# A two-block transformer layer on one Trainium2 core: squares summed on VectorE, narrow weights stationary in four column groups, router products between the last projection's units

## The reference

```
h = rmsnorm(x, norm_mix_g);  z = h @ w_in          # among its columns 8 + 8 narrow ones, a and b
g_log = -exp(a_log) * softplus(a + dt_bias);  beta = sigmoid(b)      # gated delta rule, latent attention
x = x + merged @ w_out
h = rmsnorm(x, norm_ffn_g)                                           # "norm_ffn"
x = x + (silu(conv(gate)) * conv(up)) @ w_down
x = rmsnorm(x, norm_final_g)                                         # "norm_final"
h = rms_norm(x, norm1_g);  proj = h @ w_in_2       # among its columns 32 narrow ones, dt
...                                                                  # state-space branch, windowed attention
x = x + merged @ w_out_2
h2 = rms_norm(x, norm2_g)
logits = h2 @ [w_router_group, w_router_expert]                      # 8 + 64 = 72 columns
...                                                # best group, two of its experts, 64 experts in all
x = x + sum over chosen experts of gate * ((silu(h2 @ w_gate_e) * (h2 @ w_up_e)) @ w_down_e)
```

## Time and profile before

| | |
|---|---|
| time, median of 3 runs | 1587.01 us (1586.24 to 1587.95) |
| the profiled execution's own time | 1585.9 us |
| its span, first to last instruction | 1584.0 us |
| mean granted TensorE clock | 0.98 |
| PE busy | 1487.1 us (94%) |
| DVE busy | 512.3 us (32%) |
| ACT busy | 333.8 us (21%) |
| DMA | 347.31 MB, mean 219 GB/s |

### The profile page before, as it was taken

How to read it: one execution, slowest core, us unless ns; L and a number is a source line. 1 busy time by engine, 2 the same in 40 slices (tenths; PEclk the granted TensorE clock), 3 DMA queues, 4 the chain that set the end, 5 groups by cost and what they waited for, 6 DMA issues and landing times.

```text
span 1584.0 us, 29393 instructions
## 1 busy us (share of the span) xinstructions
PE 1487.1 (94%) x12766; PEld 1257.9 (79%) x12766; DVE 512.3 (32%) x1255; ACT 333.8 (21%) x737; POOL 3.8 (0%) x6
## 2 busy tenths in 40 slices
PE   8999989999999999899999999997999888797988
PEld 7868879978888888787788888887777667576756
DVE  1435064221244420218753551013322222122212
ACT  1152321331100000112435531001111111111111
POOL 0000000000000000000000000000000000000000
PEclk9999999999999999999999999997999999999999
DMA  8333424224344324344334444393999999999992
GB/s 315 127 109 131 159 85 150 81 80 160 133 148 146 132 104 165 155 146 148 107 107 147 146 134 145 120 372 121 418 419 420 419 419 420 420 419 420 419 419 88
DMA packets 58334, 347.31 MB, mean 219 GB/s; under 512 B 12416, under 2 KB 13536, under 8 KB 18656
## 3 DMA queue, kind: packets, MB, share of 16 engines
q1 hardware_dynamic: 55536, 339.11, 55.3%
q10 hardware_dynamic: 2672, 6.33, 1.1%
HBM read 413.13 MB, written 1.49 MB: 262 GB/s over the span
## 4 chain that ended last, share of the span: by engine, by line
PE 84%; DMA 7%; DVE 4%; issue 2%; ACT 1%; SPq 0%; DVEq 0%; ACTq 0%
PE bank L375 34%; PE bank L988 9%; PE bank L419 8%; PE bank L389 6%; PE bank L1008 5%; DMA work<-w_gate_e_dram 5%; PE bank L1019 4%; PE bank L1032 3%; PE bank L435 2%; DVE work L1616 2%; DMA ring<-w_gate_e_dram 2%; PE bank L351 1%; PE bank L522 1%; PE bank L478 1%; PE bank L881 1%
## 5 line engine op out<-in xcount | busy, mean ns | idle before, releaser
L375 PE MATMUL bank<-hT,ring 128*128 128x256 f32 x2080 | 460.6, 382 | 3.4 <-DVE hT L1616 3.4
L375 PEld LDWEIGHTS bank<-hT,ring 128*128 128x128 f32 x2080 | 396.2, 192 | 63.8 <-issue 10.4
L1625 DVE TENSOR_TENSOR xT<-xT,bank 128x512 f32<-128x512 f32 x100 | 68.7, 687 | 349.6 <-PE bank L1008 231.4
L375 PE MATMUL bank<-work,ring 128*128 128x256 f32 x640 | 139.1, 379 | 0.0
L375 PEld LDWEIGHTS bank<-work,ring 128*128 128x128 f32 x640 | 121.4, 190 | 17.3 <-issue 1.0
L419 PE MATMUL bank<-work,ring 128*128 128x256 f32 x608 | 131.6, 379 | 0.0
L419 PEld LDWEIGHTS bank<-work,ring 128*128 128x128 f32 x608 | 115.5, 190 | 15.7
L988 PE MATMUL bank<-work 128*32 128x128 f32 x2240 | 99.1, 274 | 19.0 <-issue 13.9
L988 PEld LDWEIGHTS bank<-work 128*32 128x32 f32 x2240 | 90.7, 110 | 29.7 <-issue 29.3
L988 PE MATMUL bank<-ring,work 128*32 128x128 f32 x1728 | 98.9, 275 | 11.6 <-issue 7.5
L988 PEld LDWEIGHTS bank<-ring,work 128*32 128x32 f32 x1728 | 90.4, 110 | 22.2 <-issue 22.0
(11 more groups left out here) (317 smaller groups left out, 1545.0 us busy)
## 6 DMA issues: line engine op xcount, KB each, us to landing
work<-w_gate_e_dram SPq DMA_DIRECT2D x35, 1024.0 KB, 25.9
work<-w_up_e_dram SPq DMA_DIRECT2D x35, 1024.0 KB, 24.7
work<-w_down_e_dram SPq DMA_DIRECT2D x32, 1024.0 KB, 26.7
ring<-w_down_e_dram SPq DMA_DIRECT2D x27, 1024.0 KB, 25.7
ring<-w_gate_e_dram SPq DMA_DIRECT2D x25, 1024.0 KB, 26.3
ring<-w_up_e_dram SPq DMA_DIRECT2D x25, 1024.0 KB, 25.1
ring<-w_up_dram SPq DMA_DIRECT2D x22, 1024.0 KB, 4.9
hT<-w_gate_e_dram SPq DMA_DIRECT2D x22, 1024.0 KB
```

The lines of the kernel that those rows point to most:

```text
L375: m = mm(b[:, j * SEQ:(j + 1) * SEQ], w[:, k, j * P:(j + 1) * P], tile(k), start=(k == 0), stop=(k == kt - 1))
L1625: return v.tensor_tensor(dst, a, b, ALU.add)
```

## The change: what it does

- **Squares.** `residual` gets a step after its third unit: `sum_squares` on DVE adds the first six tiles of squares into one (128x512, 128x512, 128x256). `norm_sum(..., summed=True)` then needs three products in place of eight: that sum and the last two tiles. It holds for `norm_ffn`, `norm_final` and the router's sums; `norm_mix` and `norm1` stay as they were.
- **Narrow projections.** `small_features` makes the narrow weights (padded to 32 columns) stationary in four column groups of the array and streams the 256 tokens: 8 products, tile k in column group k mod 4. The four partial sums lie on 128 partitions; ACT copies them (`small_kept`), and `small_tokens` adds and transposes them with two products against a constant `fold`. That happens one unit later: after `qkv` 4 for `ab`, after `att2` 1 for `dt`. The small products `gcum` and `rows1` move behind `qkv` 5, and ACT's steps on `ab` behind the latent squares.
- **Router.** `route_pair` is called between the `out2` units: pairs 0 and 1 after units 1 and 2, pair 2 after unit 3, pair 3 at the end.

```diff
-            def norm_sum(key, kt=KD, src=sq):
+            def norm_sum(key, summed=False):
...
+                if summed:
+                    pe.wait_ge(S("squares_summed"), nth("squares_summed"))
+                    mm(b[:, 0:SEQ], ones, sq[:, 0:SEQ], start=True, stop=False)
+                    nth("squares", 3)
+                for k in range(6 if summed else 0, KD):
...
-            def small_tokens(key, w, n, src, fresh=None):
+            def small_features(key, w, src):
+
+                b = new(key, "parts")
+                pe.wait_ge(bank_free(key, "parts"), used(key, "parts") - 1)
+                for k in range(KD):
+                    j = k % 4
+                    m = mm(b[32 * j:32 * j + 32, 0:SEQ], w[:, k, :], src[:, k, :], start=(k < 4), stop=(k >= 4),
+                           tile_position=(0, 32 * j))
+                m.then_inc(product_ready, 1)
+
+            def small_tokens(key):
+
+                pe.wait_ge(bank_free(key, "parts"), used(key, "parts"))
                 b = new(key)
...
+                    m = mm(b[:, t * 32:(t + 1) * 32], small_parts[:, t * P:(t + 1) * P], con("fold"), start=True, stop=True)
...
-            small_tokens("ab", w_ab, 16, hT)
+            small_features("ab", w_ab, hT)
             to_features(("qkv", 4), "w_qkv", hT)
+            small_tokens("ab")
...
             for i in range(4):
                 to_features(("out2", i), "w_out2", merged2T, fresh=each_merged if i == 0 else None)
+                if i >= 1:
+                    route_pair(i - 1)
...
+            pe.wait_ge(S("squares_summed"), nth("squares_summed"))
+            for t in range(TT):
+                mm(ss[t][:, 0:1], sq[:, t * P:(t + 1) * P], ones[:, 0:1], start=True, stop=False)
+            route_pair(3)
+            pe.wait_ge(S("squares"), nth("squares", 4))
+            for k in (6, 7):
+                for t in range(TT):
+                    m = mm(ss[t][:, 0:1], sq[:, k * SEQ + t * P:k * SEQ + (t + 1) * P], ones[:, 0:1],
+                           start=False, stop=(k == KD - 1))
...
+                    if i == 2:
+                        sum_squares(squared)
+
+            def sum_squares(squared):
+
+                dve.wait_ge(S("squares"), squared + 3)
+                add(sq[:, 0:512], sq[:, 0:512], sq[:, 512:1024]).then_inc(S("dve_step"), 1)
+                dve.wait_ge(S("dve_step"), nth("dve_step"))
+                add(sq[:, 0:512], sq[:, 0:512], sq[:, 1024:1536]).then_inc(S("dve_step"), 1)
+                dve.wait_ge(S("dve_step"), nth("dve_step"))
+                add(sq[:, 0:SEQ], sq[:, 0:SEQ], sq[:, SEQ:512]).then_inc(S("squares_summed"), 1)
```

More of the change, by code:

```diff
@@ L392, in to_tokens @@
                 unit_read()
-            def small_tokens(key, w, n, src, fresh=None):
+            def small_features(key, w, src):
[8 more added lines that the diff above has]
+                pe.wait_ge(bank_free(key, "parts"), used(key, "parts"))
                 b = new(key)
-                if used(key) > 1:
-                    pe.wait_ge(bank_free(key), used(key) - 1)
+                pe.wait_ge(bank_free(key), used(key) - 1)
                 for t in range(TT):
[L399 to L403, removed]
+                    m = mm(b[:, t * 32:(t + 1) * 32], small_parts[:, t * P:(t + 1) * P], con("fold"), start=True, stop=True)
                 m.then_inc(product_ready, 1)
@@ L905, in _, with route_pair @@
                 split_features(("o_ssd", i), "w_ssd_out2", ysT, 16, 1)
[L906 to L912, removed]
+            first_route = len(product) + 4
+            for n in range(first_route, first_route + TT):
+                pe.wait_ge(free_sem[n % 8], n // 8)
+            def route_pair(i):
                 pe.wait_ge(S("gained"), nth("gained"))
@@ L1185, in _, with small_kept @@
             act.wait_ge(S("loads"), nth("loads", 48))
[L1187 to L1192, removed]
+            def small_kept(key):
+                act.wait_ge(product_ready, made(key, "parts"))
+                A_(small_parts, at((key, "parts"))[:, 0:SEQ], ACT.Copy).then_inc(bank_free(key, "parts"), 1)
+            small_kept("ab")
             for i in range(3):
@@ L1200, in _ @@
                 .then_inc(S("lat_squares"), 1)
+            act.wait_ge(S("sp_in"), nth("sp_in"))
+            A_(expA, row("a_log"), ACT.Exp)
+            A_(ab[:, 16:32], ab[:, 16:32], ACT.Exp, scale=-1.0)
+            A_(sp_e, sp_t, ACT.Exp).then_inc(S("act_step"), 1)
+            act.wait_ge(S("act_step"), nth("act_step"))
+            A_(sp_e, sp_e, ACT.Ln, bias=ones[:, 0:1]).then_inc(S("sp_out"), 1)
             act.wait_ge(product_ready, made("latn"))
@@ L1890, in gated, with residual @@
                 mul(merged[:, pair, :], quads(at((first, i))[:, :], 2), gA[:, pair, :]).then_inc(bank_free(first, i), 1)
[L1892 to L1904, removed]
-            def residual(name):
+            def residual(name, squared):
                 for i in range(4):
```

50 lines of the change are left out of this document (30 added, 20 removed).

## The result

| | time, us | note |
|---|---|---|
| before | 1587.4 median of 4 (1586.24 to 1587.95) | profiled execution 1585.9, span 1584.0 |
| after | 1567.18 median of 4 (1565.32 to 1569.6) | profiled execution 1567.29, span 1565.4 |
| ratio | 0.9876, 95% interval 0.9861 to 0.9892 | |

What follows compares the result with a forecast made beforehand. Transfers bound the experts' stage, whose start hangs on TensorE's path ahead of it. Savings of 3.5 + 1.8 + 2.1 + 5.1 = 12.5 us turn the profiled 1585.9 into 1573.4, a median of 1574.5 us; range 1569.5 to 1580.0.

Steps and rivals of the forecast that it cites:

- What bounds the kernel: Experts' stage: transfer-bound, its start hangs on TensorE's path; time saved ahead of 1103 us moves the end equally.
- rival C: Experts' stage: swallows the gain if transfers don't hang on the gate products; end stays at 1586 to 1587; chance 0.04.
- Part 1: Narrow products `ab` and `dt` in column groups: save 3.5 us (including the slow `qkv` unit behind) and 1.8 us.
- Part 2: Norm sums at norm_ffn and norm_final: shorter wait behind the projection saves 1.07 us, twice, 2.1 us.
- rival B: Norms: new TensorE pauses bring the clock down, each fall costing about 1.4 us; 1575.9 or 1577.3; chance 0.2.
- Part 3: Router, around `out2`: pairs between units and summed squares save 5.1 us, 3.2 of it clock; lower bound 1.9.
- Rival A: `ab` and router: clock gives little back, saving 1.4 and 3.2 us less; 7.9 us in all, 1579.1; chance 0.2.
- Sum: Whole kernel: 3.5 + 1.8 + 2.1 + 5.1 = 12.5 us saved, giving a median of 1574.5 us.

Runs made afterwards that it cites:

- b_narrow: Kernel before with only the narrow products `ab` and `dt` changed, working area at its old address; 1575.61 us, ratio 0.9936.
- b_norms: Kernel before with only the summed squares at norm_ffn and norm_final; 1585.53 us, ratio 0.9998.
- a_aligned: Kernel after, padded so that all 15 targets of the expert weights begin at multiples of 512 bytes; 1567.98 us, ratio 0.9884.
- al_fill: a_aligned plus six products on constants (24 instructions) in the pauses of the three norms; 1562.32 us, ratio 0.9849.
- b_again: Kernel before, unchanged, profiled once more; 1585.35 us, ratio 1.0005.
- b_route: Kernel before with only the router's part changed, on the old addresses; 1580.75 us, ratio 0.9970.
- b_layout: Kernel before with only the change's data sizes (padded `ab` weights, 32 more columns of constants), no product changed; 1580.91 us, ratio 0.9975.
- b_sbuf: Kernel before with 160 unused float32 per partition ahead of the working area, HBM as before; 1580.36 us, ratio 0.9969.
- a_oldaddr: Kernel after with the working area back at its old on-chip addresses, `w_ab` moved behind everything else; 1570.29 us, ratio 0.9909.

## Why the prediction was right and wrong

**What bounds the kernel, the step that failed.** "A microsecond taken off TensorE's path ahead of 1103 moves the end by a microsecond", and with it "the stretch from there to the end as long as before (1584.0 - 1103.5 = 480.5)". The first half held: nothing of the upstream gain was swallowed, and rival C is false. The second did not: from the gate on, the stage went from 480.6 to 471.3 us. That term was put at nothing, and it is the step that failed. It treated a stage that the diff doesn't touch as one that can't change, and the text says only that it would be wrong "if that last stretch grows". Two side effects of the edits made up the 9.3 us. The diff widens a buffer allocated ahead of eight of the weights' slots (6.5 us by the address), and the products taken out make the list ahead of the stage shorter (2.8 us behind that). The earlier trace rows gave the rate, 419 GB/s at a DMA share of 1.01; it was read as a ceiling of the transfers, and it held only for slots at those addresses.

**Part 1.** Right. `ab`: 3.6 us where 3.5 were forecast; the column-group products take 1.00 us (0.9 forecast), the fold 0.36 (0.48), the unit behind 7.10 at a granted clock of 1.00. No trace with the four groups has the fall; seven of eight with the 16-column products do, so the 1.4 us of clock in this term are likely and not certain. `dt`: 1.9 for 1.8. The latents' scaling hid, as forecast. On its own (b_narrow) the part came with 3.5 us more at places that it doesn't touch, which the sum had no term for.

**Part 2.** The mechanism was right, the size was off, and its rival decided. The term was 1.07 each and measured 0.88 and 0.89: the last four instructions take 1.15 us in place of 0.87; why is not shown. Then rival B took 1.7 us of the 1.8 back in `up1`; the 0.2 at norm1 is within what the unchanged kernel shows there (5.17 and 6.76). On its own the part is worth nothing (b_norms), and rival B had 0.2 for a chance; four of five traces with these pauses showed it. The Trainium skill (TensorE: Matmul & The Clock Gate, Part 1) says that the gate follows how busy TensorE has been, and a_aligned against al_fill agrees here: products on constants in the pause keep the clock at 1.00. At 34 to 38 us of the trace of before it doesn't: TensorE was busy 2.00 of 2.00 us on 16-column products and fell to 0.51.

**Part 3.** Right in sum and in parts: 5.1 us; last sum 3.1 us behind the end of `out2` (1066.87 to about 1070.0; 3.2 forecast); units between the pairs 6.96 and 6.97. But the clock fall was only put off, to 0.50 from 1075 to 1077, and 0.9 us was lost between the router and the gate: 0.3 in the gather products (6.29 for 6.00), 0.6 in the wait ahead of them.

**Rival A** was partly true, and not of the change: b_again's router took 3.1 us more than b_route's where the first trace said 5.1, since the fall came later in it. So 2.0 us of Part 3's gain hang on the trace that was read.

**Sum.** Upstream 9.3 for 12.5, nearly all of the difference in `up1`, behind the router and in the scatter of the start. Downstream 9.3 for nothing. Two errors of opposite sign; the uncosted one was three times the other. That the upstream parts add up as well as they do is in part luck, as clock falls come and go between executions of one kernel (`ab`, norm1, router).

## What to carry to other kernels

When an edit changes the size of a buffer, look at what is allocated behind it: in a stage whose DMA share is 1, the address of the target alone was worth 5 to 7 us of 1584 in the stage and 4 to 6 in the median, as much as the whole rebuilding of the router, and a padding of 128 bytes bought it. Which address is good can't be told from these runs; try a few. A saving ahead of a pause should be costed together with the clock behind the pause, and a few products on constants in it are cheap insurance: 5.7 us for 24 instructions here. Last, count the instructions that a change takes out of the busiest engine's list, look in the chain for "issue" of 1 to 3 us at fixed counts behind the last transfer, and expect some microseconds either way from where they fall.

## What the runs showed of the hardware that was not expected

- With the eight slots of the working area 128 bytes beyond a multiple of 256 bytes per partition the weights moved at 419 to 420 GB/s, with them at multiples of 256 at 424, and with all fifteen at multiples of 512 at 425. The other six slots at 128 bytes beyond cost at most 1 GB/s, so this is not a rule about a slot's start alone. The source in HBM made no difference (b_layout and b_sbuf differ by 0.2 us in the stage).
- TensorE stopped 1.6 to 2.6 us, at times up to 3.4 (a_oldaddr), at fixed places in its list while the transfers filled the DMA engines, and at 79 of 82 stops of 1.4 us or more went on 1.2 to 1.6 us after a packet of the kind "instruction" had ended. The same 128 instructions added ahead cost 3.4 us in one kernel and gained 4.8 in another.
- Behind sixteen-column products back to back, TensorE busy 2.00 of 2.00 us, the clock fell from 2.4 to 1.2 GHz in seven of eight traces; behind 32-column weights in four groups for 1.00 us it did in none of six.
- 256-column float32 instructions in four column groups took 0.0625 us each (1.00 for 16), where full-width ones take 0.218.
